# Hybrid gMLP and RG-LRU decoder step: output transposes of the first token half inside the last K unit, two of their copies on VectorE

## What is computed

```python
def trunk(x, conv_hist, h0, norm_gains, ...):
    for li in range(DEPTH):
        g = norm_gains[li]
        hn = rms_norm(x, g[0])
        m = gmlp_mixer(hn, ...) if li % 2 == 0 else rglru_mixer(hn, ...)
        x = x + rms_norm(m, g[1])
        f = swiglu(rms_norm(x, g[2]), ffn_w_in[li], ffn_w_out[li])
        x = x + rms_norm(f, g[3])
    return x, new_conv, new_h, v_rows
```

## Time and profile before

| | |
|---|---|
| median of 3 runs | 1508.67 us (1508.56 to 1508.69) |
| profiled execution | 1508.73 us, span of its instructions 1507.2 us |
| TensorE clock granted | 1.000 |
| TensorE busy | 1498.5 us, 99% of the span |
| VectorE busy | 968.6 us, 64% |
| ScalarE busy | 689.6 us, 46% |
| GpSimd busy | 214.2 us, 14% |
| written to HBM | 3.29 MB |

### The profile page before, as it was taken

How to read it: one execution, slowest core, us unless ns; L and a number is a source line. 1 busy time by engine, 2 the same in 40 slices (tenths; PEclk the granted TensorE clock), 3 DMA queues, 4 the chain that set the end, 5 groups by cost and what they waited for, 6 DMA issues and landing times.

```text
span 1507.2 us, 27754 instructions
## 1 busy us (share of the span) xinstructions
PE 1498.5 (99%) x10922; PEld 1481.2 (98%) x10922; DVE 968.6 (64%) x1350; ACT 689.6 (46%) x1131; POOL 214.2 (14%) x173
## 2 busy tenths in 40 slices
PE   9999999999999999999999999999999999999998
PEld 8999999999999999999999999999999999999998
DVE  6454577667344588777764438889588877755444
ACT  5244432324343444655553435286563555554433
POOL 0100033333000002121110000505002111210002
PEclk9999999999999999999999999999999999999999
DMA  7322232322222212423332323212222333333211
GB/s 242 106 74 72 76 110 79 96 86 90 82 84 84 84 44 71 112 83 111 84 110 83 95 68 94 85 44 91 87 60 85 84 96 99 83 99 98 82 60 68
DMA packets 171568, 133.55 MB, mean 89 GB/s; under 512 B 4920, under 2 KB 149584, under 8 KB 171348
## 3 DMA queue, kind: packets, MB, share of 16 engines
q1 hardware_dynamic: 169812, 128.30, 28.5%
q0 software_dynamic: 1664, 3.95, 1.0%
HBM read 128.92 MB, written 3.29 MB: 88 GB/s over the span
## 4 chain that ended last, share of the span: by engine, by line
PE 98%; DVE 1%; ACT 0%; DMA 0%; issue 0%; SPq 0%; POOLq 0%; POOL 0%; ACTq 0%
PE ps L568 97%; DVE hl L1875 0%; PE ps L634 0%; DMA wide<-in_x_prompt_dram 0%; ACT hh L1312 0%; DVE wlo L1887 0%; DVE yb L1812 0%; POOLq L81 0%; POOL xT L2293 0%; PE ps L1029 0%; PE ps L718 0%; DVE acc L1554 0%; DVE hl L1577 0%; ACT whi L1054 0%; DVE wide L1915 0%
## 5 line engine op out<-in xcount | busy, mean ns | idle before, releaser
L568 PE MATMUL ps<-hh,whi 128*128 128x288 f32 x2624 | 642.5, 297 | 0.0
L568 PE MATMUL ps<-hh,wlo 128*128 128x288 f32 x2624 | 637.5, 295 | 0.0
L568 PE MATMUL ps<-hl,whi 128*128 128x288 f32 x2624 | 637.5, 295 | 0.0
L568 PEld LDWEIGHTS ps<-hh,whi 128*128 128x128 f32 x2624 | 446.7, 188 | 2.2 <-DVE wlo L1537 0.2
L568 PEld LDWEIGHTS ps<-hh,wlo 128*128 128x128 f32 x2624 | 447.5, 188 | 0.0
L568 PEld LDWEIGHTS ps<-hl,whi 128*128 128x128 f32 x2624 | 447.4, 188 | 0.0
L1054 ACT ACTIVATE whi<-stage 128x1024 fp32r<-128x1024 f32 (+2 forms) x176 | 174.4, 999 | 377.8 <-PE ps L568 377.8
L1537 DVE TENSOR_TENSOR wlo<-stage,whi 128x1024 fp32r<-128x1024 f32 (+2 forms) x176 | 208.6, 1190 | 205.3 <-ACT whi L1054 205.0
L568 PE MATMUL ps<-eh,whi 128*128 128x288 f32 x512 | 151.6, 296 | 0.3 <-DVE wlo L1887 0.3
L568 PE MATMUL ps<-el,whi 128*128 128x288 f32 x512 | 151.1, 295 | 0.0
L568 PE MATMUL ps<-eh,wlo 128*128 128x288 f32 x512 | 150.6, 294 | 0.0
(11 more groups left out here) (201 smaller groups left out, 1562.7 us busy)
## 6 DMA issues: line engine op xcount, KB each, us to landing
stage<-in_ffn_w_in_dram SPq DMA_DIRECT2D x88, 512.0 KB, 4.0
stage<-in_ffn_w_out_dram SPq DMA_DIRECT2D x40, 512.0 KB, 3.9
stage<-in_gm_w_in_dram SPq DMA_DIRECT2D x32, 384.0 KB, 3.5
stage<-in_gm_w_in_dram SPq DMA_DIRECT2D x24, 512.0 KB, 3.8
stage<-in_gm_w_out_dram SPq DMA_DIRECT2D x24, 512.0 KB, 3.8
stage<-in_rg_w_in_dram SPq DMA_DIRECT2D x16, 512.0 KB, 3.8
stage<-in_rg_w_out_dram SPq DMA_DIRECT2D x8, 512.0 KB, 3.9
wide<-in_x_prompt_dram SPq DMA_DIRECT2D x4, 512.0 KB, 7.1
```

The lines of the kernel that those rows point to most:

```text
L568: return pe.matmul(out, w, x, start=start, stop=stop, skip_group_check=more)
```

## The change

Four edits of the tail, the arithmetic stays the same.

1. All 16 transposes of half 0 (`turn_out(0, k)`, k 0 to 7) move into the last projection: in group 1, half 1, last unit (`j == per - 1`), behind tile 0. Tiles 1 to 3 of this unit, 18 matmuls, follow them.
2. The state transposes move behind `post_spread`, and wait for ScalarE's first two output copies; ScalarE copies the states behind two of its own pieces as before, but these are now pieces 2 and 3.
3. The pieces 0 and 1 are copied by VectorE, behind the second and the third `post_add` of half 1's last group.
4. Piece 3 is gathered in bank 6 (it was 7), piece 6 in bank 7 (it was 6). `turn_out(1, k)` waits for VectorE's two copies too. The wait for `out_act >= 3` stands unchanged; ScalarE's third output copy was piece 2's and is now piece 4's.

```diff
-        OUT_BANK = [0, 2, 4, 7, 1, 5, 6, 0, 2, 4]
+        OUT_BANK = [0, 2, 4, 6, 1, 5, 7, 0, 2, 4]
...
         def out_by_act(b):
 
-            return b != 8
+            return b not in (0, 1, 8)
...
                                     if m == 2:
                                         post_spread(p, 0)
+                                if name == "FO1" and (G, h, j, m) == (1, 1, per - 1, 0):
+                                    pe.wait_ge(t_ready, count_t(p, 0, KD - 1))
+                                    for k in range(KD):
+                                        turn_out(0, k)
...
-            pe.wait_ge(t_ready, count_t(POST["FO1"], 0, KD - 1))
-            for k in range(4):
-                turn_out(0, k)
             post_sums(POST["FO1"], 1)
             for m in range(4):
                 pe.wait_ge(pair_free[m], free0["END"][m])
+            post_spread(POST["FO1"], 1)
+            pe.wait_ge(out_act, 2)
             for k in range(KD):
                 last = pe.transpose(ps[0:36, 5 + k // 4, (k % 4) * P:(k % 4 + 1) * P], sout[:, k, :], ident[:, :])
             last.then_inc(so_turned, 1)
-            post_spread(POST["FO1"], 1)
-            for k in range(4, KD):
-                turn_out(0, k)
             pe.wait_ge(so_copied, 1)
+            pe.wait_ge(out_dve, 2)
             for k in range(KD):
                 if k == 4:
                     pe.wait_ge(out_act, 3)
...
             for b in range(2 * NT):
-                if b == 2:
+                if b == 4:
                     act.wait_ge(so_turned, 1)
...
+            def copy_piece(b):
+                dve.wait_ge(out_turned, b + 1)
+                dve.tensor_copy(out_tile(b), out_bank(b)).then_inc(out_dve, 1)
+
             for m in range(4):
                 post_add(p, 1, 1, m)
+                if m in (1, 2):
+                    copy_piece(m - 1)
...
-            for b in range(2 * NT):
-                if not out_by_act(b):
-                    dve.wait_ge(out_turned, b + 1)
-                    dve.tensor_copy(out_tile(b), out_bank(b)).then_inc(out_dve, 1)
+            copy_piece(8)
```

More of the change, by code:

```diff
@@ L775, in _, with turn_out @@
             mix(DG // P - 1, FG - 1, 1, GRP - 1)
+            def turn_out(h, k):
+                pe.wait_ge(x_last[0 if x_by_dve(h, k) else 1], x_made(h, k))
+                for b, (hf, c) in enumerate(PIECES):
+                    if hf == k // 4 and (c >= 2) == (h == 1):
+                        r = P if c < NC else TS
+                        last = pe.transpose(out_bank(b)[:, (k % 4) * P:(k % 4 + 1) * P],
+                                            xT[:, k, c * P:c * P + r], ident[:, :])
+                        if k % 4 == 3:
+                            last.then_inc(out_turned, 1)
             def out_phase(name):
```

## The result

The changed kernel takes 1513.23 us (median of 7 runs, 1512.62 to 1513.91), the kernel before on the same chip 1508.58 (1507.96 to 1508.79): a ratio of 1.0032, 95% interval 1.0023 to 1.0041. It is 4.65 us slower, where 2.0 were forecast, and outside the range.

The account below looks back on a forecast made before the run. TensorE, busy for 99% of the span, and a closing chain without slack were taken as the bound. 1.83 + 0.38 - 0.18 = +2.03 on 1508.73 gave 1510.76, on the median 1510.7; range 1509.5 to 1511.9.

Parts of the forecast that it names:

- Part 1: Last unit of the last projection: 16 transposes at 0.109 us spacing, plus 0.09 for returning to large matmuls, +1.83 us.
- rival A: Last unit of the last projection: transposes don't pipeline, 4.50 us instead of 1.74, giving 1513.5; chance 0.07.
- Part 2: VectorE, between the additions: two copies, each occupying 0.61 us, make the last addition late on the chain, +0.38 us.
- Part 3: Between sums and spread: with the state transposes gone, the spread starts earlier, -0.18 us.
- Part 4: Behind the spread: later state transposes and copy start the second half's k 0 0.45 late, slack used up, 0 lost.
- Part 5: Ahead of k 4: waiting for ScalarE's third copy, now piece 4, starts it some 0.25 late, 0 lost, margin 0.15.
- Part 6: SyncE's stores at the end: later state transfers don't delay piece 4, earlier writes buy nothing, 0.
- Rival C: End of the kernel: writes rather than the chain hold it, early exit returns 1.0 to 1.5, 1509.2 to 1509.7; chance 0.06.
- Rival B: Tail: a state copy 0.3 to 1 us later holds the second half up, 1510.9 to 1511.7; chance 0.11.
- the second stretch: From the square of tile 0 to the first normed tile of the second half; what the forecast sum priced, at 2.03.

Follow-up runs that it names:

- the run of this part alone: Kernel before with only the 16 transposes moved into the last K unit: 1510.92 us; with 6 and 10 discarded products added: 1509.98 us.
- the stretches filled: Changed kernel with 9, 4 and 8 discarded products of 288 columns in TensorE's three idle stretches: 1510.35 us, ratio 1.0013 to the kernel before.
- the later stretches filled: Changed kernel with 4 and 8 discarded products in the two later idle stretches only, the one behind the last large matmul left idle: 1511.67 us.

## Why the prediction was wrong

**Part 1, the 16 transposes: right.** Predicted +1.83. From the first of them to the next large matmul 1.66 us (1491.69 to 1493.35), and the 0.09 of the return (1493.35 to 1493.57, against 0.13): 1.75. The spacing was 0.104 us. Together with the run of this part alone (1.75 more from the square of tile 0 to the first normed tile) nothing is left for rival A: the Trainium skill's 275 ns (TensorE: Matmul & The Clock Gate, Part 4: PE-mode transpose) isn't the spacing here. That the measured 1513.23 lies close to that rival's 1513.5 is a coincidence.

**Part 2, the copies on VectorE: right.** Predicted +0.38. The additions of tile 1 and tile 3 lie 1.94 apart (1494.88 to 1496.82) instead of 2 x 0.80: +0.34. Each copy occupied 0.60.

**Part 3, the earlier spread: wrong, by 0.17.** From the reciprocal to the first normed tile it takes 1.24 (1498.32 to 1499.56), before 1.25 (1496.00 to 1497.25). With TensorE waiting, the spread starts 0.32 behind the reciprocal's start instead of 0.40 and takes longer itself (0.88 against 0.81). With the stretches filled it starts 0.23 behind it, and the first normed tile comes 0.08 earlier than before, not 0.18. The state transposes ahead of the spread had cost next to nothing.

**Part 4, the late states: the step that failed.** It said "8 transposes (1.04)" and "12 x 0.109 + 0.17", slack used up, 0. The structure was right: k 0 waited for the state copy, and with the clock held it started 0.44 late (forecast 0.45), with nothing lost behind it. What failed is the durations, which were those of a clock of 1.00: the prediction took it that the granted clock would stay there when TensorE's new idle time stood in the chain. Measured: 1.66 and 2.82, and from the first normed tile to the last copies +1.99. With the clock held the same links cost 0.00.

**Part 5, the third copy: right in effect.** A wait of 0.26 in the changed kernel. With the clock held it was 0.47, k 4 started 0.27 late (forecast 0.25), and the last copies weren't late.

**Part 6, SyncE and the writes: right.** 4.3 us from the last copies to the end, 4.4 before. Rival C fell with it.

**Rival B** had the right place, and the state copy was indeed late, by 0.59. But its cause was the clock, not a wait on ScalarE, and so the price of 0.2 to 1.0 missed the slow transposes behind the copy. The rule that led to the true one was on the table, as the second half of what was quoted from the Trainium skill (TensorE: Matmul & The Clock Gate, Part 4: PE-mode transpose) ahead of the prediction's rivals: transposes don't hold the clock up. I answered it with the kernel before, where the clock stood at 1.00 through transposes. That row was taken with TensorE at work in the very stretch, 1493.85 to 1495.00, that the change empties: I counted the 8 transposes there as free and didn't ask what their going would leave. The rule itself isn't what the runs show: transposes as fillers kept the clock (1510.53 against 1513.23). The Trainium skill has the general rule on the same page (TensorE: Matmul & The Clock Gate, What's actually happening), that TensorE's clock is held down unless its activity releases it. The changed kernel's trace agrees (1.33, 0.65 and 1.11 us of idle, and 0.50), and so do the filled runs.

In sum: 2.07 of the second stretch forecast as 2.03, and 1.99 of clock forecast as 0; in the medians, each against the kernel before measured with it, 1.96 with the clock held and 2.69 on top without. The second is more than 1.99 at least in part because other executions lost more than the profiled one (1512.90, the second fastest of seven); they have no profile.

## What to carry to other kernels

Work that is hidden in a wait of TensorE may still have a use: it keeps the clock. Before moving hidden work out of a wait, write down what idle time it leaves and price what follows at half the clock too, above all where slack was just found to be zero. And when a tail's runs scatter by 1 to 2 us, sort them by the execution's granted clock first, and look for two groups in the times themselves, since a mean clock of 0.999 can stand for either; discarded products in the gaps are a quick way to tell a clock loss from a wait.

## What was not expected of the hardware

- 21 discarded products of 288 columns in three idle stretches made the kernel 2.9 us faster (1513.23 to 1510.35; 2.7 if each is set against the kernel before measured with it), and 25 discarded transposes nearly as much (1510.53). Transposes of 128 columns held TensorE's clock here as products did.
- The clock doesn't come back with the first work: in the changed kernel it stood at 0.50 from within 1499 to 1500 until within 1506 to 1507, through most of the 8 state transposes and most of the 24 behind them.
- One kernel has two times: with the later stretches filled, 4 executions took 1509.9 to 1510.0 and 7 took 1511.5 to 1511.9, with a mean clock of 1.000 and of 0.998 to 0.999. What decides it within a kernel, and at what instant the clock falls, stays open.
- The 8 transposes of the kernel before were not only free, they filled a wait; but emptying that wait alone (1.09 us, with another of 1.08 further on) didn't bring the clock down in the profiled execution.
